# Sixteen up pairs of the first MLP by seven products instead of fifteen, with half of the factor sums' operands in PSUM

## The chip, the cores and the metric

The kernel runs on one core of one Trainium2 chip. The metric is the device time of one execution in microseconds (us), the median of several runs. Lower is better. The kernel is a hand-scheduled program: every engine has its own instruction list, and the lists are tied together by semaphores alone.

## The reference, cut to what matters

Three transformer layers run over 512 tokens of width 1024, in float32. The change touches the up projection of the first layer's MLP:

```
h2 = rms_norm(x, ffn_norm)                             # 512 x 1024
u = causal_dwconv(h2 @ w_up, conv_w, conv_b)           # w_up 1024 x 5632, three taps along the tokens
a, bval = jnp.split(u, 2, axis=-1)                     # 2816 + 2816 columns
return x + (jax.nn.silu(a) * bval) @ w_down            # w_down 2816 x 1024
```

Everything is computed with float32 accuracy. Each operand is split into a high and a low part (fp32r), and a product is the sum high x high + high x low + low x high: three matmuls for one.

## The kernel before

The 2816 columns of `a` and the 2816 of `bval` make 22 *pairs* of 128-column tiles (one tile of `a`, one of `bval`). Activations lie transposed, 128 features on the partitions and 512 tokens along the free axis.

**Plain pairs.** The first `N_PLAIN` = 7 pairs run as two ordinary tiles each (`up_tile`): 8 blocks of 128 features x 3 matmuls of 512 columns, 48 matmuls a pair. The weight tile arrives by DMA in `stage`, ScalarE (ACT) copies it to `w_hi` (L1791), GpSimd (POOL) subtracts to get `w_lo` (L639), VectorE (DVE) multiplies the result by `rstd` (`scaled`, L2890), ACT applies the first convolution tap (`conv_0_of`, L2055), and DVE the other two (`conv`, L2897 and L2900).

**Pairs by seven products.** The other `Q_UP` = 15 pairs use Strassen's scheme (Winograd's form) on 2 x 2 blocks: the pair's two tiles are the rows, two halves of the 1024 features the inner blocks, two halves of the tokens (256 each) the columns. `up_product(q, k)` runs one of the seven products, in the order `UP_ORDER` = A11, S1, A12, S2, S4, A22, S3: 4 feature blocks x 3 matmuls of 256 columns, so 12 matmuls a product and 84 a pair. Some products accumulate in the PSUM region of an earlier one, so they wait for ACT to copy that region away: S2 for `p1_copied` (L2094), S4 for `p5_copied` (L2101), S3 for `u2_copied` (L2107). DVE then adds the pieces (`c_00`, `c_01` at L2981, `c_1` at L2988).

**Factors.** The activation side of the seven products, the *factors* (four blocks B11, B12, B21, B22 of the normed input and sums T1 to T4 of them; seven of the eight are used), is made once during the plain pairs, in four *columns* k = 0 to 3, at the plain pairs i in `FACTORS_AT = [0, 1, 3, 4]`. For each column DVE computes blocks and sums (`factors_first`, `factors_second`), ACT copies them to the high parts (`factor_highs`), and DVE and POOL subtract to get the low parts (both have a `factor_lows`). After the last column DVE makes the weight sums of the first product pair (`up_sum`, L2947 and on).

**Weights of the product pairs.** Pair q's raw weights (two loads of 512 KB) go to `stage` for odd q and to other buffers for even q. The load of pair q waits for POOL's low part of A22 of pair q - 2.

**Hand-over to the down projection.** After the last pair the down projection uses `stage` again. Its first loads wait as this line says (L604):

```
sp.wait_ge(slot_low, UP_LOW_AT[HI_A22, Q_UP - 1 - (Q_UP % 2)])
loads(T_DOWN1, T_QKV[0])
```

In the last pair's turn, ACT's list has the high part of the first down tile (`down_split_hi(T_DOWN1)`, L2131) ahead of `p5_copied`, and that of the second down tile and three parts `f_high` (L2122) ahead of `u2_copied`. The down projection's first output tile (d = 0) takes its operands as they are finished: high parts first, then POOL's low parts of the down tiles (L762), then DVE's low parts of the MLP's hidden values (`f_low`, L2996).

Of the kernel before, what the change touches and what calls it, by code (L numbers as in the profile page):

```python
# [16 lines left out]
F32 = mybir.dt.float32  # L17
F32R = mybir.dt.float32r
ALU = mybir.AluOpType
# [3 lines left out]
S = 512  # L23
# [28 lines left out]
N_PLAIN = 7  # L52
# [27 lines left out]
FACTORS = [F_B11, F_T1, F_B21, F_T2, F_B22, F_T3, F_T4]  # L80
N_HIGH = N_PROD + 1
# [30 lines left out]
F_FREE = [F_B11, F_T1, F_B21, F_T2, F_B22, F_T4, F_T3]  # L112
# [60 lines left out]
def program(nc, x_in, params, consts, buckets, swa_table, weights, pairs, tables, out):  # L173
    with ExitStack() as ctx:
# [138 lines left out]
        SUM_X, SUM_Y = TR[1], OB  # L313

# [318 lines left out]
        def _(pool):  # L633
# [90 lines left out]
            def factor_lows(k):  # L724
# [4 lines left out]
                if k < QUADS - 1:  # L729
                    nc.gpsimd.tensor_tensor(factor[:, F_T1:, 1, ks], e[:, 2 * S:].rearrange("p (c s) -> p c s", c=4),  # L730
                                            factor[:, F_T1:, 0, ks].bitcast(F32), ALU.subtract).then_inc(factor_low, 1)
                    return
                nc.gpsimd.tensor_tensor(factor[:, F_T1, 1, ks], e[:, 2 * S:2 * S + HS], factor[:, F_T1, 0, ks].bitcast(F32),
                                        ALU.subtract).then_inc(factor_low, 1)
                if N_PLAIN - 2 in FACTORS_AT:
                    up_low(HI_A11, 0)
                nc.gpsimd.tensor_tensor(factor[:, F_T3:, 1, ks], e[:, 2 * S + HS:].rearrange("p (c s) -> p c s", c=3),
                                        factor[:, F_T3:, 0, ks].bitcast(F32), ALU.subtract).then_inc(factor_low, 1)
# [120 lines left out]
        def _(pe):  # L859
# [409 lines left out]
            def up_product(q, k):  # L1269
# [3 lines left out]
                f = FACTORS[k]  # L1273
# [10 lines left out]
                elif k == HI_S1:  # L1284
                    if q == 0:
                        pe.wait_ge(factor_low, QUADS)
                    else:
                        pe.wait_ge(product_added, 4 * (q - 1) + C_01)
                elif k == HI_A12 and q:
                    pe.wait_ge(product_added, 4 * (q - 1) + C_10)  # L1290
                elif k == HI_S2:
                    pe.wait_ge(up_moved, moved_at(q, P1_COPY))
                    if q == 0:
                        pe.wait_ge(factor_low, X_LOWS)
                elif k == HI_S4:
                    pe.wait_ge(up_moved, moved_at(q, P5_COPY))
                elif k == HI_A22:
                    pe.wait_ge(product_added, 4 * q + C_00)
# [485 lines left out]
        def _(act):  # L1784
# [261 lines left out]
            root(1)  # L2046
            def conv_0_of(i, p_):
# [15 lines left out]
            def factor_highs(k):  # L2063
# [3 lines left out]
                act.activation(factor[:, F_B11, 0, ks], factor_parts[k % 2][:, 0:HS], ACT.Copy).then_inc(ffh_ready, 1)  # L2067
                act.activation(factor[:, F_B21:, 0, ks], factor_parts[k % 2][:, S:].rearrange("p (c s) -> p c s", c=6),
# [1702 lines left out]
```

## Time and profile before

| | us |
|---|---|
| median of 3 runs (lowest to highest) | 1697.94 (1697.69 to 1698.26) |
| the profiled execution's own time | 1697.71 |
| its span, first to last instruction | 1695.6 |
| PE (TensorE matmul) busy | 1687.2 of 1695.6 |
| PEld (weight loads) busy | 1458.4 |
| DVE / ACT / POOL busy | 1135.2 / 901.3 / 1024.6 |

The profile is one execution. An engine's busy time counts the instructions that do work. Matmuls overlap one another in the profile, so the time that one really costs is the distance between two starts, not its own duration. The granted TensorE clock is 0.999 of full speed over the span.

### The profile page before, as it was taken

What the parts mean: (1) busy time and instruction counts of PE and PEld (TensorE: products, weight loads), DVE (VectorE), ACT (ScalarE), POOL (GpSimd) and SP (SyncE); (2) the same over time, 40 slices, a digit from 0 to 9 for tenths busy, and PEclk for the clock granted to TensorE, in tenths of its full rate; (3) what the DMA queues carried; (4) which work ended last, traced back from release to release, by engine and by line L of the source; (5) the groups of instructions that cost most, each with busy time, mean ns of one, the idle gap of its engine ahead of it and who ended that gap; (6) DMA issues with size and microseconds to landing.
All of it is one profiled execution on the core that took longest, in us unless ns stands there. A gap on an engine that the chain in (4) does not pass through costs nothing.

```text
span 1695.6 us, 28204 instructions
## 1 busy us (share of the span) xinstructions
PE 1687.2 (100%) x9959; PEld 1458.4 (86%) x9959; DVE 1135.2 (67%) x2222; ACT 901.3 (53%) x1643; POOL 1024.6 (60%) x1077
## 2 busy tenths in 40 slices
PE   9999999999999999999999999999999999999998
PEld 7778889999888888888989898977777889898988
DVE  6875788887411455667766666777777675757576
ACT  6665546787423444335454544656565454535355
POOL 6543688778554443357575757755554666666666
PEclk9999999999999999999999999999999999999999
DMA  5222343322234322223323233232331243333332
GB/s 196 74 69 63 100 125 103 110 100 88 87 100 143 97 69 84 75 87 112 112 88 112 89 111 92 98 125 84 119 106 50 88 136 100 100 100 99 101 99 76
DMA packets 48523, 168.22 MB, mean 99 GB/s; under 512 B 5216, under 2 KB 6512, under 8 KB 48400
## 3 DMA queue, kind: packets, MB, share of 16 engines
q1 hardware_dynamic: 48112, 166.08, 30.6%
q8 instruction: 73, 1.20, 0.3%
q10 hardware_dynamic: 288, 0.53, 0.1%
q14 instruction: 50, 0.41, 0.1%
HBM read 164.35 MB, written 2.24 MB: 98 GB/s over the span
## 4 chain that ended last, share of the span: by engine, by line
PE 99%; DVE 0%; ACT 0%; issue 0%; DVEq 0%
PE bank L961 19%; PE bank L880 7%; PE bank L879 7%; PE bank L885 7%; PE bank L1729 6%; PE bank L1738 6%; PE bank L1730 6%; PE bank L1311 3%; PE bank L1304 3%; PE bank L1303 3%; PE bank L979 3%; PE bank L980 3%; PE bank L985 3%; PE bank L1362 2%; PE bank L1353 2%; PE bank L1355 2%
## 5 line engine op out<-in xcount | busy, mean ns | idle before, releaser
L639 POOL TENSOR_TENSOR w_lo<-stage,w_hi 128x256 fp32r<-128x256 f32 x664 | 528.2, 827 | 416.2 <-ACT w_hi L1791 218.2
L1791 ACT ACTIVATE w_hi<-stage 128x1024 fp32r<-128x1024 f32 x166 | 174.7, 1053 | 167.0 <-DMA stage<-weights 57.3
L880 PE MATMUL bank<-xn_lo,w_hi 128*128 128x512 f32 x544 | 211.7, 389 | 0.0
L879 PE MATMUL bank<-xn_hi,w_hi 128*128 128x512 f32 x544 | 211.7, 389 | 0.0
L961 PE MATMUL bank<-xn_hi,w_hi 128*128 128x512 f32 x464 | 188.8, 407 | 0.0
L961 PE MATMUL bank<-xn_lo,w_hi 128*128 128x512 f32 x464 | 181.8, 392 | 0.0
L3480 DVE TENSOR_TENSOR x_space<-x_space,bank 128x256 f32<-128x256 f32 (+1 forms) x217 | 96.9, 455 | 86.8 <-PE bank L1738 84.9
L1738 PE MATMUL bank<-arena 128*128 128x256 f32 x896 | 146.6, 283 | 0.0
L885 PE MATMUL bank<-xn_hi,w_lo 128*128 128x512 f32 x544 | 135.0, 389 | 0.0
L1729 PE MATMUL bank<-arena 128*128 128x256 f32 x512 | 128.8, 283 | 0.0
L1730 PE MATMUL bank<-arena 128*128 128x256 f32 x512 | 128.7, 283 | 0.0
L1738 PEld LDWEIGHTS bank<-arena 128*128 128x128 f32 x896 | 124.8, 192 | 0.0
L961 PE MATMUL bank<-xn_hi,w_lo 128*128 128x512 f32 x464 | 123.8, 398 | 0.0
L885 PEld LDWEIGHTS bank<-xn_hi,w_lo 128*128 128x128 f32 x544 | 102.1, 188 | 21.2
L880 PEld LDWEIGHTS bank<-xn_lo,w_hi 128*128 128x128 f32 x544 | 102.1, 188 | 21.1
L879 PEld LDWEIGHTS bank<-xn_hi,w_hi 128*128 128x128 f32 x544 | 102.2, 188 | 20.9
L3500 DVE TENSOR_TENSOR arena<-tmp,arena 128x256 fp32r<-128x256 f32 (+2 forms) x120 | 108.2, 922 | 3.8 <-ACT arena L2514 2.5
L961 PEld LDWEIGHTS bank<-xn_hi,w_hi 128*128 128x128 f32 x464 | 87.2, 188 | 22.9 <-issue 6.3
L961 PEld LDWEIGHTS bank<-xn_hi,w_lo 128*128 128x128 f32 x464 | 84.6, 188 | 21.7 <-issue 4.9
L961 PEld LDWEIGHTS bank<-xn_lo,w_hi 128*128 128x128 f32 x464 | 87.3, 188 | 16.0
L1729 PEld LDWEIGHTS bank<-arena 128*128 128x128 f32 x512 | 98.3, 192 | 0.1
L1730 PEld LDWEIGHTS bank<-arena 128*128 128x128 f32 x512 | 98.3, 192 | 0.0
(512 smaller groups left out, 4317.5 us busy)
## 6 DMA issues: line engine op xcount, KB each, us to landing
stage<-weights SPq DMA_DIRECT2D x189, 512.0 KB, 3.5
stage<-pairs SPq DMA_DIRECT2D x46, 512.0 KB, 3.6
prob<-pairs SPq DMA_DIRECT2D x32, 512.0 KB, 3.6
bias<-table SPq DMA_DIRECT2D x11, 896.0 KB, 5.5
xn_raw<-pairs SPq DMA_DIRECT2D x14, 512.0 KB, 4.4
out<-y SPq DMA_DIRECT2D x8, 256.0 KB, 2.3
x_space<-x_in SPq DMA_DIRECT2D x3, 512.0 KB, 7.3
bias<-swa_table SPq DMA_DIRECT2D x4, 256.0 KB, 3.7
```

What stands on the lines that cost most here:

```text
L639: ins = nc.gpsimd.tensor_tensor(w_lo[:, p_, ks], stage[:, p_, ks], w_hi[:, p_, ks].bitcast(F32), ALU.subtract)
L879: pe.matmul(G[p_][:], w_hi[:, p_, k], hi[:, k], start=(first and k == ks[0]), stop=False)
L880: mm = pe.matmul(G[p_][:], w_hi[:, p_, k], lo[:, k], start=False, stop=False)
L885: mm = pe.matmul(G[p_][:], w_lo[:, p_, k], hi[:, k], start=False, stop=(last and k == ks[-1]))
L961: mm = pe.matmul(G[p_][:], (w_hi if i < 2 * KD else w_lo)[:, p_, k], (xn_lo if i < 2 * KD and i % 2 else xn_hi)[:, k], start=(i == 0), sto ...
L979: pe.matmul(G[dd][:], w, ff_hi[:, k], start=(k == k0), stop=False)
L1729: pe.matmul(region, w, fc_hi[:, i, f], start=(fresh and i == 0), stop=False, skip_group_check=True)
L1730: pe.matmul(region, w, fc_lo[:, i, f], start=False, stop=False, skip_group_check=True)
L1738: mm = pe.matmul(region, w, fc_hi[:, i, f], start=False, stop=(i == QUADS - 1), skip_group_check=True)
L1791: act.activation(w_hi[:, p_], stage[:, p_], ACT.Copy).then_inc(hi_ready, 1)
L3480: dve.tensor_tensor(dst, dst, src, ALU.add).then_inc(product_added, 1)
L3500: dve.tensor_tensor(fc_lo[:, i, a:b + 1].rearrange("p c s -> p (c s)"), src, fc_hi[:, i, a:b + 1].rearrange("p c s -> p (c s)").bitcast(F3 ...
```

## The change

`N_PLAIN` goes from 7 to 6, so 16 pairs run by products and 6 plain. The plain stage, under which the factors are made, is one pair shorter, while `FACTORS_AT` stays. The making of the factors is rearranged:

- ACT copies `rstd` once to an idle PSUM bank (`ROOT`). DVE's blocks read it there.
- B12 (needed only on the way) and T1, T2 are written to PSUM (`B12`, `T12`) instead of SBUF, so that each block or sum has at most one tensor operand in SBUF. `T12` and `B12` are one buffer each, where the SBUF parts alternate between two.
- The factors lie in another order (`U_...`), with T1 and T2 first. DVE makes the low parts of T1, T2 and B11, POOL those of the other four. PE's waits on them move accordingly.

The diff, cut to its core:

```diff
-N_PLAIN = 7
+N_PLAIN = 6
+U_T1, U_T2, U_B11, U_B21, U_B22, U_T3, U_T4 = range(7)
+UP_FACTORS = [U_B11, U_T1, U_B21, U_T2, U_B22, U_T3, U_T4]
-F_FREE = [F_B11, F_T1, F_B21, F_T2, F_B22, F_T4, F_T3]
+F_FREE = [UP_FACTORS[k] for k in UP_ORDER]
+        ROOT, T12, B12 = MB, OB, TR[0][:, 0:HS]
...
             root(1)
+            act.wait_ge(rstd_ready, 2)
+            act.activation(ROOT[:], rstd[:], ACT.Copy)
...
             def factor_highs(k):
-                act.activation(factor[:, F_B11, 0, ks], factor_parts[k % 2][:, 0:HS], ACT.Copy).then_inc(ffh_ready, 1)
-                act.activation(factor[:, F_B21:, 0, ks], factor_parts[k % 2][:, S:].rearrange("p (c s) -> p c s", c=6),
+                act.activation(factor[:, U_T1:U_T2 + 1, 0, ks], T12.rearrange("p (c s) -> p c s", c=2), ACT.Copy).then_inc(ffh_ready, 1)
+                act.activation(factor[:, U_B11:, 0, ks], factor_parts[k % 2][:, 0:5 * HS].rearrange("p (c s) -> p c s", c=5),
                                ACT.Copy).then_inc(ffh_ready, 1)
...
             def factors_first(k):
-                dve.scalar_tensor_tensor(out=e[:, 0:S], in0=x[:, k], scalar=pcol("ffn_norm", k, k + 1), in1=rstd[:],
+                dve.scalar_tensor_tensor(out=b11, in0=x[:, k, 0:HS], scalar=pcol("ffn_norm", k, k + 1), in1=ROOT[:, 0:HS],
                                          op0=ALU.mult, op1=ALU.mult)
-                dlink(dve.scalar_tensor_tensor(out=e[:, S:2 * S], in0=x[:, k + 4], scalar=pcol("ffn_norm", k + 4, k + 5), in1=rstd[:],
+                dve.scalar_tensor_tensor(out=B12, in0=x[:, k, HS:S], scalar=pcol("ffn_norm", k, k + 1), in1=ROOT[:, HS:S],
+                                         op0=ALU.mult, op1=ALU.mult)
+                dlink(dve.scalar_tensor_tensor(out=e[:, HS:3 * HS], in0=x[:, k + 4], scalar=pcol("ffn_norm", k + 4, k + 5), in1=ROOT[:],
                                                op0=ALU.mult, op1=ALU.mult))
-                dve.tensor_tensor(t1, b12, b11, ALU.subtract)
-                dlink(dve.tensor_tensor(t3, b22, b12, ALU.subtract))
+                dve.tensor_tensor(t1, B12, b11, ALU.subtract)
+                dlink(dve.tensor_tensor(t3, b22, B12, ALU.subtract))
```

The wait of L604 is not in the diff, but its value follows from `Q_UP`. With 15 pairs it names pair 13; with 16 it names pair 15, the last, whose raw weights now lie in `stage`.

**DVE, the last factor column.** Before, the two blocks and the sums T1, T3, then `scaled`, then T2, T4, one more convolution (two rows of `tmp<-bank,par,tmp`), a `scaled`, and the low parts:

```order
L2916 SCALAR_TENSOR_TENSOR v_tok<-x_space,par,rstd 128x512 [waits factor_low,ff_ready,ffh_ready]
L2918 SCALAR_TENSOR_TENSOR v_tok<-x_space,par,rstd 128x512
L2920 TENSOR_TENSOR v_tok<-v_tok 128x256 [waits dve_chain]
L2921 TENSOR_TENSOR v_tok<-v_tok 128x256
L2890 TENSOR_TENSOR bank<-bank,rstd 128x512 [waits tile_done,dve_chain]
L2926 TENSOR_TENSOR v_tok<-v_tok 128x256
L2927 TENSOR_TENSOR v_tok<-v_tok 128x256 [waits dve_chain]
L2897 SCALAR_TENSOR_TENSOR tmp<-bank,par,tmp 128x511 [waits conv_0]
L2900 SCALAR_TENSOR_TENSOR tmp<-bank,par,tmp 128x510 [waits conv_1]
L2890 TENSOR_TENSOR bank<-bank,rstd 128x512 [waits tile_done]
L2933 TENSOR_TENSOR arena<-v_tok,arena 128x256 [waits ffh_ready]
L2936 TENSOR_TENSOR arena<-v_tok,arena 128x2x256 [waits ffh_ready]
```

The same place in the changed kernel:

```order
L2922 SCALAR_TENSOR_TENSOR v_tok<-x_space,par,bank 128x256 [waits factor_low,ff_ready,ffh_ready]
L2924 SCALAR_TENSOR_TENSOR bank<-x_space,par,bank 128x256
L2926 SCALAR_TENSOR_TENSOR v_tok<-x_space,par,bank 128x512
L2928 TENSOR_TENSOR bank<-bank,v_tok 128x256 [waits dve_chain]
L2929 TENSOR_TENSOR v_tok<-v_tok,bank 128x256
L2896 TENSOR_TENSOR bank<-bank,rstd 128x512 [waits tile_done,dve_chain]
L2934 TENSOR_TENSOR bank<-v_tok,bank 128x256
L2935 TENSOR_TENSOR v_tok<-v_tok,bank 128x256 [waits dve_chain]
L2941 TENSOR_TENSOR arena<-bank,arena 128x2x256 [waits ffh_ready]
L2944 TENSOR_TENSOR arena<-v_tok,arena 128x256 [waits ffh_ready]
L2954 TENSOR_TENSOR bank<-bank,arena_raw 128x512 [waits ff_ready,quad_full0,slot_high]
```

The first block is in two pieces, all sums have a bank among their operands, and the convolution and `scaled` that stood between the sums and the low parts now come after the weight sums, whose first is the last row.

**ACT, the third factor column.** Before, its high parts (the two rows of `arena`) stand ahead of the next weight tile's high part:

```order
L2055 ACTIVATE tmp<-bank,par 128x512 [waits f_made,up_moved]
L2067 ACTIVATE arena<-arena_raw 128x256 [waits factor_made]
L2068 ACTIVATE arena<-arena_raw 128x6x256
L1791 ACTIVATE w_hi<-stage 128x1024 [waits hi_free,stage_full0]
L2055 ACTIVATE tmp<-bank,par 128x512 [waits f_made,up_moved]
```

In the changed kernel they stand behind it:

```order
L2061 ACTIVATE tmp<-bank,par 128x512 [waits f_made,up_moved]
L1795 ACTIVATE w_hi<-stage 128x1024 [waits hi_free,stage_full0]
L2073 ACTIVATE arena<-bank 128x2x256 [waits factor_made]
L2074 ACTIVATE arena<-arena_raw 128x5x256
L2061 ACTIVATE tmp<-bank,par 128x512 [waits f_made,up_moved]
```

So these high parts wait for the weight tile, too.

**SP, the loads from the last product pairs to the first down tiles.** Before (`stage<-pairs` and `xn_raw<-pairs` are the raw weights of odd and even pairs, the branch carries the wait of L604):

```order
L597 DMA stage<-pairs 128x1024 [waits slot_low]
L597 DMA stage<-pairs 128x1024
L597 DMA xn_raw<-pairs 128x1024 [waits slot_low]
L597 DMA xn_raw<-pairs 128x1024
L507 UNCONDITIONAL_BRANCH [waits slot_low]
L507 ISA
L504 ISA [waits lo_ready]
L504 DMA stage<-weights 128x1024
```

In the changed kernel:

```order
L600 DMA xn_raw<-pairs 128x1024 [waits slot_low]
L600 DMA xn_raw<-pairs 128x1024
L600 DMA stage<-pairs 128x1024 [waits slot_low]
L600 DMA stage<-pairs 128x1024
L510 UNCONDITIONAL_BRANCH [waits slot_low]
L510 ISA
L507 ISA [waits lo_ready]
L507 DMA stage<-weights 128x1024
```

The last pair's loads now go to `stage`, right ahead of the down tiles that take the same buffer.

## Rows read from the trace of the kernel before

**Rows 1.** The page's span, and the chain that ended last, by engine.

```profile
span 1695.6 us, 28204 instructions
...
PE 99%; DVE 0%; ACT 0%; issue 0%; DVEq 0%
```

**Rows 2.** Timeline of PE (start, duration): last plain pair's start, first product's start.

```profile
261.72 0.39 PE L1261 MATMUL bank<-xn_hi,w_hi 128*128 128x512 f32 x1
...
272.60 0.28 PE L1303 MATMUL bank<-arena,bias_slots 128*128 128x256 f32 x1
```

**Rows 3.** Timeline of PE: first matmuls of product pairs 3, 4 and 14 (the last).

```profile
302.83 0.28 PE L1303 MATMUL bank<-arena,bias_slots 128*128 128x256 f32 x1
...
312.91 0.28 PE L1303 MATMUL bank<-arena,bias_slots 128*128 128x256 f32 x1
...
413.71 0.28 PE L1303 MATMUL bank<-arena,bias_slots 128*128 128x256 f32 x1
```

**Rows 4.** Timeline of DVE, from the last factor column to the first product.

```profile
249.59 1.30 DVE L2916 SCALAR_TENSOR_TENSOR v_tok<-x_space,par,rstd 128x512 f32<-128x512 f32 x1
...
252.64 0.84 DVE L2920 TENSOR_TENSOR v_tok<-v_tok 128x256 f32<-128x256 f32 x1
...
255.96 2.51 DVE L2927 TENSOR_TENSOR v_tok<-v_tok 128x256 f32<-128x256 f32 x1
...
261.37 1.78 DVE L2936 TENSOR_TENSOR arena<-v_tok,arena 128x512 fp32r<-128x512 f32 x1
...
265.11 0.69 DVE L2947 TENSOR_TENSOR bank<-bank,arena_raw 128x512 f32<-128x512 f32 x1
...
272.80 0.70 DVE L2890 TENSOR_TENSOR bank<-bank,rstd 128x512 f32<-128x512 f32 x1 [0.27 <-PE bank L1266]
```

**Rows 5.** Timeline of ACT, from the third factor column to the first product pair.

```profile
244.69 1.47 ACT L2068 ACTIVATE arena<-arena_raw 128x1536 fp32r<-128x1536 f32 x1
246.38 1.06 ACT L1791 ACTIVATE w_hi<-stage 128x1024 fp32r<-128x1024 f32 x1 [0.22 <-DMA stage<-weights]
...
277.08 0.38 ACT L2101 ACTIVATE bank<-bank 128x256 f32<-128x256 f32 x1
```

**Rows 6.** Timeline of POOL: the last low part it makes before the first product.

```profile
270.82 1.29 POOL L745 TENSOR_TENSOR v_split<-arena_raw,v_split 128x512 fp32r<-128x512 f32 x1
```

**Rows 7.** The first two down loads: SP's timeline; line L504's and L597's landings; SP's waits.

```profile
404.72 0.88 SPq L504 DMA_DIRECT2D stage<-weights  x2
...
DMA to landing us min/median/max: 4.6/4.9/5.3
...
DMA to landing us min/median/max: 3.5/4.0/4.5
...
SPq L507 <- POOL xn_hi L745: 8.7, 1, 8.7
```

**Rows 8.** Timeline of ACT in the last product pair.

```profile
416.29 1.06 ACT L2131 ACTIVATE arena<-stage 128x1024 fp32r<-128x1024 f32 x1
418.05 0.37 ACT L2101 ACTIVATE bank<-bank 128x256 f32<-128x256 f32 x1 [0.70 <-issue]
418.33 1.05 ACT L2131 ACTIVATE arena<-stage 128x1024 fp32r<-128x1024 f32 x1
...
420.84 0.38 ACT L2107 ACTIVATE rstd<-bank 128x256 f32<-128x256 f32 x1
```

**Rows 9.** Timelines of DVE, of POOL and of PE behind it; PE's wait there.

```profile
421.25 0.43 DVE L2981 TENSOR_TENSOR bank<-rstd,bank 128x256 f32<-128x256 f32 x1 [2.54 <-ACT rstd L2107]
...
424.41 0.43 DVE L2988 TENSOR_TENSOR bank<-xn_raw,bank 128x256 f32<-128x256 f32 x1 [0.19 <-ACT xn_raw L2113]
...
429.52 4.63 POOL L762 TENSOR_TENSOR bias_slots<-stage,bias_slots 128x256 fp32r<-128x256 f32 x4
...
434.24 1.63 PE L1362 MATMUL bank<-arena,bias_slots 128*128 128x512 f32 x6
...
PEld bank L1362 <- POOL bias_slots L762: 0.2, 1, 0.2
```

More of the change, by code:

```diff
@@ L729, in factor_lows @@
                 if k < QUADS - 1:
[L730 to L731 removed]
+                    nc.gpsimd.tensor_tensor(factor[:, U_B21:, 1, ks], e[:, HS:5 * HS].rearrange("p (c s) -> p c s", c=4),
+                                            factor[:, U_B21:, 0, ks].bitcast(F32), ALU.subtract).then_inc(factor_low, 1)
                     return
[L733 to L734 removed]
+                nc.gpsimd.tensor_tensor(factor[:, U_B21:U_B22 + 1, 1, ks], e[:, HS:3 * HS].rearrange("p (c s) -> p c s", c=2),
+                                        factor[:, U_B21:U_B22 + 1, 0, ks].bitcast(F32), ALU.subtract).then_inc(factor_low, 1)
                 if N_PLAIN - 2 in FACTORS_AT:
                     up_low(HI_A11, 0)
[L737 to L738 removed]
+                nc.gpsimd.tensor_tensor(factor[:, U_T3:, 1, ks], e[:, 3 * HS:5 * HS].rearrange("p (c s) -> p c s", c=2),
+                                        factor[:, U_T3:, 0, ks].bitcast(F32), ALU.subtract).then_inc(factor_low, 1)
             def up_low(k, q):
@@ L1284, in up_product @@
                 elif k == HI_S1:
+                    if q:
+                        pe.wait_ge(product_added, 4 * (q - 1) + C_01)
+                elif k == HI_A12:
                     if q == 0:
@@ L1287, in up_product @@
                     else:
-                        pe.wait_ge(product_added, 4 * (q - 1) + C_01)
-                elif k == HI_A12 and q:
-                    pe.wait_ge(product_added, 4 * (q - 1) + C_10)
+                        pe.wait_ge(product_added, 4 * (q - 1) + C_10)
                 elif k == HI_S2:
                     pe.wait_ge(up_moved, moved_at(q, P1_COPY))
-                    if q == 0:
-                        pe.wait_ge(factor_low, X_LOWS)
                 elif k == HI_S4:
@@ L1297, in up_product @@
                 elif k == HI_A22:
+                    if q == 0:
+                        pe.wait_ge(factor_low, X_LOWS)
                     pe.wait_ge(product_added, 4 * q + C_00)
@@ L2905, in parts @@
                 e = factor_parts[k % 2]
-                return [e[:, c * HS:(c + 1) * HS] for c in range(8)]
+                return [e[:, c * HS:(c + 1) * HS] for c in range(5)] + [T12[:, 0:HS], T12[:, HS:S]]
             def factors_first(k):
                 e = factor_parts[k % 2]
+                b11, b21, b22, t3, t4, t1, t2 = parts(k)
                 if k >= 2:
@@ L2932, in factor_lows @@
                 dve.wait_ge(ffh_ready, 2 * k + 1)
-                dve.tensor_tensor(factor[:, F_B11, 1, ks], e[:, 0:HS], factor[:, F_B11, 0, ks].bitcast(F32),
+                dve.tensor_tensor(factor[:, U_T1:U_T2 + 1, 1, ks], T12.rearrange("p (c s) -> p c s", c=2),
+                                  factor[:, U_T1:U_T2 + 1, 0, ks].bitcast(F32), ALU.subtract).then_inc(ff_ready, 1)
+                dve.wait_ge(ffh_ready, 2 * k + 2)
+                dve.tensor_tensor(factor[:, U_B11, 1, ks], e[:, 0:HS], factor[:, U_B11, 0, ks].bitcast(F32),
                                   ALU.subtract).then_inc(ff_ready, 1)
-                dve.wait_ge(ffh_ready, 2 * k + 2)
-                dve.tensor_tensor(factor[:, F_B21:F_T1, 1, ks], e[:, S:2 * S].rearrange("p (c s) -> p c s", c=2),
-                                  factor[:, F_B21:F_T1, 0, ks].bitcast(F32), ALU.subtract).then_inc(ff_ready, 1)
             def up_sum(q, k):
```

8 lines of the change are left out of this document (3 added, 5 removed).

## The prediction

> **What bounds the kernel now.** I read the page first. The chain that ended last is PE at 99% [rows 1]: matmul follows matmul almost without a gap. So a change can gain only by what it takes out of PE's own list, and it loses whatever it makes PE wait. Next I read PE's timeline for the price of the two kinds of pair, then the timelines of DVE, ACT and POOL at the two seams: from the plain pairs to the products (around 272.6 us), and from the last pair to the down projection (from 413.7 us). Those are the only places where the order around PE changes.
>
> **What PE's list gains.** The last plain pair starts at 261.72 and the first product at 272.60 [rows 2]: 10.88 us for 48 matmuls, 0.227 us each. A pair by products goes from 302.83 to 312.91 [rows 3]: 10.08 us for 84 matmuls, 0.120 us each. One pair changes kind, so PE's list is 0.80 us shorter. This is all that can be gained.
>
> The Trainium skill (page "TensorE: Matmul & The Clock Gate", section "Back-to-back issue gap") gives N / 2.4 + 2.5 ns for an isolated matmul of N columns at full clock. By it a plain pair is 48 x 215.8 ns and a product pair 84 x 109.2 ns, and the gain would be 10.36 - 9.17 = 1.19 us. The trace's spacings are wider, above all for 256 columns (120 against 109 ns), so the measured 0.80 decides. The same section warns that at smaller N the spacing also carries the weight load, which is what the rows look like.
>
> **Seam 1, plain pairs to products.** Products would now start at 261.72 instead of 272.60, 10.88 us sooner, while the last factor column still belongs to plain pair 4. In the kernel before, DVE started on that column at 249.59, ended its low parts at 261.37 + 1.78 = 263.15, made the first weight sum at 265.11, and was done with the work behind it so that it waited 0.27 us for PE at 272.80 [rows 4]. Left as it was, the column would be ready only after the products want it.
>
> The new column costs less. A 256-wide sum with both operands in SBUF took 0.84 and even 2.51 us [rows 4]; one with a bank among its operands took 0.43 [rows 9]. So four sums take 1.7 us. The blocks (two of 256, one of 512) I take at about 0.45 + 0.45 + 0.75, an estimate from 0.43 for 256 and 0.70 for 512 with a bank operand [rows 4, 9]. With the `scaled` between them (0.7) and about 0.2 for the links, 249.59 leads to about 253.8 for the finished sums; before it was 255.96 + 2.51 = 258.47. ACT's first high part (some 0.6 for 512 columns) and DVE's low part (0.7) follow, then ACT's second part and DVE's low part of B11. That puts the first weight sum at about 255.6 to 256.5, and it is earlier still if the column starts sooner than 249.59. The start is set by the high parts of the third column: they now stand behind a weight tile's copy that waits until PE has freed `w_hi`. That is PE's second half of pair 4, near 243.3 by PE's pace, so they run from about 244.4 to 246.2, against 244.69 + 1.47 = 246.16 before [rows 5]. The order change there costs nothing, and the column starts at about 248.5 to 249.6. I take 255.3 for the first weight sum, 6.4 us ahead of the first product; before it was 272.60 - 265.11 = 7.5 ahead. DVE is thus 1.1 later against PE (bounds 0.6 and 1.8).
>
> Who waits for it? After the sums DVE has the same work as before until the last `scaled`. That one had 0.27 to spare, so it is 0.8 late. ACT's copy for S4 ended at 277.08 + 0.38 = 277.46 [rows 5], 4.86 us after the first product's start; S4 starts 4 x 12 x 0.120 = 5.76 after it. That is 0.90 of cover for 0.8 of delay: cost 0, with bounds 0 and 0.8. POOL's last low part before the first product, for S4, ended at 270.82 + 1.29 = 272.11 [rows 6]; in the changed kernel I expect it 1 to 2 us behind the first product, and S4's low matmuls want it 6.7 behind: cost 0. The copy of `rstd` to the bank (ACT, 0.6) delays a weight tile that PE wants only after two plain tiles: cost 0. Fewer sums in SBUF also take less of POOL's time, which helps only engines that are not the bound.
>
> **Seam 2, last pair to the down projection.** The first two down loads go to `stage`. With 15 pairs they waited for pair 13's A22, that is, they were released one pair early: issued at 404.72 [rows 7], which is 1.09 after pair 13's start (413.71 - 10.08 = 403.63). SP was waiting for just this POOL operation [rows 7]. With 16 pairs the wait names the last pair. Call its start T: the loads leave at T + 1.09. Those two landed 4.6 and 5.3 after issue [rows 7], so the first is there at T + 5.7.
>
> ACT's list holds the copy of that tile ahead of the copy for S4. Before, it ran at 416.29, T + 2.58 [rows 8]. Now it runs at T + 5.7, 3.1 later, and the next instruction on ACT starts about 0.95 behind it, at T + 6.65. The 0.37 of `p5_copied` [rows 8] brings T + 7.05. S4 wanted it at T + 5.76: **PE stalls 1.3 us**.
>
> Next is S3, which waits for `u2_copied`. That stood 420.84 - 418.05 = 2.79 behind `p5_copied` [rows 8], so it runs from T + 9.45 to T + 9.85. S3 starts at 8.64 + 1.3 = T + 9.94: no further stall. But DVE's `c_01`, at 421.25 or T + 7.54 before [rows 9], moves to T + 9.9, 2.4 later. `c_1`, which had 0.19 to spare [rows 9], is 2.2 later, and behind it stand the last convolution, the last hidden value and POOL's low part of the third down tile (429.52 + 4.63 = 434.15 [rows 9]). PE already waited 0.2 for that part at 434.24 [rows 9], so there is no cover left, and the whole 2.2 arrives at PE. It contains the 1.3: **seam 2 costs 2.2 us in total**. Bounds: if the load lands after 3.5, the least that a pair's load took [rows 7], everything is 1.1 less, so 1.1; at 5.3 it is 2.9. Below, no bound but 0, if ACT's list had room.
>
> **The sum.** -0.80 + 0 + 2.2 = +1.4 us. The profiled execution took 1697.71 us, 2.1 more than its span; it would take 1699.1. The median of the runs shown is 0.23 higher, so I forecast 1699.3. That is 0.08% slower: below the 0.2% (3.4 us) that a measurement of this kernel can tell from no change.
>
> **The rivals.**
> *The hand-over is hidden* (chance 0.18). The loads land quickly, or ACT and DVE catch up, and the stall is 1.1 or less: -0.80 to +0.3, 1697.1 to 1698.2. For it: fast landings of 3.5 occur. Against: the loads of this very place took 4.6 and more, and PE's cover behind it was 0.
>
> *The factors come late* (0.15), which ends slower. This is one mechanism: the last column's chain DVE, ACT, DVE does not shrink as estimated, because B11's low part still has both operands in SBUF, the links between dependent sums cost more, or the third column's high parts run later than 246.2. If nothing shrank, the first weight sum would come some 9 + 3 us after 249.59, near 262, 7.8 later against PE than before, and the stall would be 7.8 - 0.27 - 0.90 = 6.6: 1706. It decides (slower by over 3.4 together with seam 2) when seam 1 costs over 2.0, when the first weight sum comes later than about 257.4. For it: the 2.51 of one sum [rows 4]. Against: 0.43 for each operation with a bank [rows 9].
>
> The Trainium skill (page "SBUF — State Buffer", section "SBUF: two separate sides") says that DVE with two SBUF inputs and GpSimd exclude each other for a whole instruction. By that rule the new sums are free of POOL, but B11's low part is not and can wait out one POOL instruction.
>
> *Faster by over 0.2%* (0.02): PE's list gives 0.80, and no wait of PE that the change could remove is near 2.6 us.
>
> **How the numbers follow.** My forecast (seam 2 between 1.1 and 2.9, seam 1 below 1) has 0.62, from +0.3 to +3.1 us. Both small costs together reaching the bound without passing it have 0.03. Within 0.2%: 0.62 + 0.18 + 0.03 = 0.83; slower 0.15, faster 0.02. The range leaves out little of the hidden case at the bottom (1697.2) and reaches a step into late factors at the top (1702.0).
>
> **What the profile of the changed kernel would show.** Right: first product at 261.7 to 262; product pairs 10.08 apart; first weight sum near 255.3; S4 of the last pair starting 7.1 instead of 5.8 us after the pair's first matmul, with ACT idle before the first L2137 until a DMA; PE waiting at the third down tile's low part for 0.9. Wrong: a gap at the first products' S1, A12 or S4 (factors late), ACT's first down copy at T + 3 to T + 4.5 (load hidden), or a PE wait in between that no row of before shows.

## The result, and the profile after

| | before | changed |
|---|---|---|
| median, us (lowest to highest, 11 runs each) | 1698.01 (1697.69 to 1699.52) | 1701.56 (1700.89 to 1703.05) |
| profiled execution's own time / its span | 1697.71 / 1695.6 | 1701.56 / 1699.8 |

The ratio is 1.002, with a 95% interval of 1.0012 to 1.0028. The change makes the kernel 3.55 us slower, which is 0.21%, right at the 0.2% that the measurement can tell from no change. The forecast was 1699.3, in a range of 1697.2 to 1702.0, with 0.83 for a difference within 0.2% and 0.15 for slower; the measured one lies on that border.

The page of the changed kernel: its span, the busy times, and the chain that ended last, by engine.

```profile
span 1699.8 us, 28304 instructions
...
PE 1688.0 (99%) x9995; PEld 1459.8 (86%) x9995; DVE 1128.0 (66%) x2234; ACT 907.8 (53%) x1654; POOL 1020.6 (60%) x1074
...
PE 96%; DVE 1%; ACT 1%; DMA 1%; POOL 0%; issue 0%; DVEq 0%; SPq 0%; ACTq 0%; POOLq 0%
```

DVE has 7 us less to do than before, and PE's share of the chain has fallen from 99% [rows 1] to 96%: the chain now leaves PE for DVE, ACT and a DMA. So PE waits where it did not. PE's timeline (start, duration, and in brackets the idle time before the row with what ended it) shows where. First the seam from plain tiles to products; S2 starts at 267.15 and S4 at 269.51.

```profile
262.32 0.28 PE L1307 MATMUL bank<-arena,bias_slots 128*128 128x256 f32 x1
...
267.15 0.36 PE L1307 MATMUL bank<-arena,bias_slots 128*128 128x256 f32 x1 [0.36 <-ACT rstd L2100]
...
269.51 0.36 PE L1307 MATMUL bank<-arena,v_split 128*128 128x256 f32 x1 [0.69 <-ACT bank L2107]
```

Then the last pair (its first matmul, and S4's), and the low part of the third down tile:

```profile
415.17 0.28 PE L1307 MATMUL bank<-arena,bias_slots 128*128 128x256 f32 x1
...
422.33 0.36 PE L1307 MATMUL bank<-arena,v_split 128*128 128x256 f32 x1 [1.24 <-ACT bank L2107]
...
438.30 1.65 PE L1366 MATMUL bank<-arena,bias_slots 128*128 128x512 f32 x6 [0.70 <-POOL bias_slots L765]
```

Distances between first matmuls, read from PE's timelines of both kernels (good to about 0.01), give this account. T is the start of the last pair, d = 0 and d = 1 are the down projection's output tiles.

| | before | changed | difference |
|---|---|---|---|
| last plain pair against a pair by products | 10.88 | 10.08 | -0.80 |
| place where the products (before: the last plain pair) start | 261.72 | 262.32 | +0.60 |
| pair 0 | 10.08 | 11.57 | +1.49 |
| pair 1 | 10.08 | 10.24 | +0.16 |
| pairs 2 to the last but one, each | 10.08 | 10.08 | 0 |
| last pair, T to down projection | 10.08 | 11.54 | +1.46 |
| d = 0 to d = 1 | 15.12 | 16.25 | +1.13 |

The sum is +4.04 (4.06 by the two starts of d = 1; the rest is rounding); the spans differ by 4.2. The 0.60 looks like scatter: three profiles of the kernel before have the first product at 272.60, 272.78 and 273.02, which less 10.88 is 261.72 to 262.14, and all the kernels here with six plain pairs have it between 261.70 and 262.46. Without it 3.44 remain, and the medians differ by 3.55. Seam 1 costs 1.65 and seam 2 2.59, against a gain of 0.80.

**Seam 1 in the changed kernel.** DVE's timeline, to be held against [rows 4]: the first sum and the last, the low parts of T1 and T2, that of B11, the first weight sum, and the last `scaled`.

```profile
250.95 0.43 DVE L2928 TENSOR_TENSOR bank<-bank,v_tok 128x256 f32<-128x256 f32 x1
...
252.80 0.42 DVE L2935 TENSOR_TENSOR v_tok<-v_tok,bank 128x256 f32<-128x256 f32 x1
253.89 0.69 DVE L2941 TENSOR_TENSOR arena<-bank,arena 128x512 fp32r<-128x512 f32 x1 [0.67 <-ACT arena L2073]
255.05 2.19 DVE L2944 TENSOR_TENSOR arena<-v_tok,arena 128x256 fp32r<-128x256 f32 x1 [0.47 <-ACT arena L2074]
257.37 0.70 DVE L2954 TENSOR_TENSOR bank<-bank,arena_raw 128x512 f32<-128x512 f32 x1
...
264.71 0.69 DVE L2896 TENSOR_TENSOR bank<-bank,rstd 128x512 f32<-128x512 f32 x1
```

POOL's timeline over the same microseconds, and ACT's copy for S4:

```profile
254.55 2.40 POOL L733 TENSOR_TENSOR arena<-arena_raw,arena 128x1024 fp32r<-128x1024 f32 x1
```

```profile
268.98 0.38 ACT L2107 ACTIVATE bank<-bank 128x256 f32<-128x256 f32 x1
```

The sums are as cheap as forecast (0.43, 0.42), and they end at 253.2. But B11's low part, a 256-wide operation whose two operands both lie in SBUF, took 2.19 us. It started 0.50 after a POOL instruction of 2.40 us and ended 0.29 after it. The first weight sum then comes 262.32 - 257.37 = 4.95 ahead of the first product; it was 7.49 before, and 6.4 in the forecast. (Two of the kernels below leave this place as it is: there the same row took 2.18 and 2.17, and pair 0 11.54 and 11.55.) The last `scaled` is 264.71 - 262.32 = 2.39 behind the first product, where it was 0.20 [rows 4]. That is 2.19 late. The copy for S4 ends 7.04 behind, where it was 4.86 [rows 5]: 2.18 late, against a cover of 0.90. The 1.28 that is left, and 0.1 to 0.2 for PE's restart, make the 1.49.

**Seam 2 in the changed kernel.** SP's timeline of the first two down loads, and their landings (line L507 between 415 and 420):

```profile
416.25 0.88 SPq L507 DMA_DIRECT2D stage<-weights  x2
...
DMA to landing us min/median/max: 4.6/4.9/5.3
```

ACT's timeline, to be held against [rows 8], and DVE's (`c_1`, and two low parts of hidden values) and POOL's (the second down tile's low part, and the third's) behind it, against [rows 9]:

```profile
420.85 1.06 ACT L2137 ACTIVATE arena<-stage 128x1024 fp32r<-128x1024 f32 x1 [2.98 <-DMA stage<-weights]
421.81 0.37 ACT L2107 ACTIVATE bank<-bank 128x256 f32<-128x256 f32 x1
...
424.62 0.36 ACT L2113 ACTIVATE rstd<-bank 128x256 f32<-128x256 f32 x1
```

```profile
427.97 0.42 DVE L2995 TENSOR_TENSOR bank<-xn_raw,bank 128x256 f32<-128x256 f32 x1
...
428.63 1.84 DVE L3003 TENSOR_TENSOR arena<-arena_raw,arena 128x512 fp32r<-128x512 f32 x2
```

```profile
426.03 3.29 POOL L765 TENSOR_TENSOR arena<-stage,arena 128x256 fp32r<-128x256 f32 x4
...
433.63 4.62 POOL L765 TENSOR_TENSOR bias_slots<-stage,bias_slots 128x256 fp32r<-128x256 f32 x4
```

The loads leave at T + 1.08, ACT's down copy starts at T + 5.68, the copy for S4 at T + 6.64, and S4 itself at T + 7.16. `c_1` is at T + 12.80 instead of T + 10.70, 2.10 late, and POOL's low part of the third tile ends at T + 23.08 instead of T + 20.44, 2.64 late. DVE's row between them accounts for the other 0.54. In the kernel before it read

```profile
425.08 1.29 DVE L2996 TENSOR_TENSOR arena<-arena_raw,arena 128x512 fp32r<-128x512 f32 x2
```

and stood behind the end of POOL's second low part (424.78). Now it starts before that end (426.03 + 3.29 = 429.32) and takes 1.84 instead of 1.29: the first of its two instructions, with both operands in SBUF, takes 1.23 instead of 0.69. It is the same meeting as at seam 1. No run takes this one away by itself.

### The profile page after: what moved, and what is told of

The parts are those of the page before. It is cut to its first block, busy times and chain, and to the rows that moved or that the text cites. A ratio compares the mean times of both kernels' runs of the same rounds, so it can differ in the third digit from the quotient of the medians.

```text
span 1699.8 us, 28304 instructions
## 1 busy us (share of the span) xinstructions
PE 1688.0 (99%) x9995; PEld 1459.8 (86%) x9995; DVE 1128.0 (66%) x2234; ACT 907.8 (53%) x1654; POOL 1020.6 (60%) x1074
## 4 chain that ended last, share of the span: by engine, by line
PE 96%; DVE 1%; ACT 1%; DMA 1%; POOL 0%; issue 0%; DVEq 0%; SPq 0%; ACTq 0%; POOLq 0%
PE bank L964 19%; PE bank L883 7%; PE bank L882 7%; PE bank L888 7%; PE bank L1733 6%; PE bank L1742 6%; PE bank L1734 6%; PE bank L1307 3%; PE bank L1315 3%; PE bank L1308 3%; PE bank L982 3%; PE bank L988 3%; PE bank L983 3%; PE bank L1366 2%; PE bank L1359 2%; PE bank L1357 2%
## 5 line engine op out<-in xcount | busy, mean ns | idle before, releaser
L642 POOL TENSOR_TENSOR w_lo<-stage,w_hi 128x256 fp32r<-128x256 f32 x656 | 519.6, 824 | 418.7 <-ACT w_hi L1795 212.3
```

Source lines behind the costliest of these rows:

```text
L642: ins = nc.gpsimd.tensor_tensor(w_lo[:, p_, ks], stage[:, p_, ks], w_hi[:, p_, ks].bitcast(F32), ALU.subtract)
```

## The experiments

Eight edited kernels and two further profiles of the kernel before. Times are medians. The experiments ran on three chips, and each ratio is against runs of the kernel before on the same chip: its medians there were 1698.66 (25 runs), 1698.38 (27) and 1698.94 (13). Medians from different chips are compared with care. The runs of the kernel before lie mostly in two groups, around 1697.9 and around 1699.3, on every chip. What makes the two groups is the last experiment's subject.

### The two halves of the change apart

The rearranged factors without the 16th pair:

```diff
-N_PLAIN = 6
+N_PLAIN = 7
```

> The changed kernel with seven plain pairs again, so only the factor sums are rearranged. My theory: both seams keep the cover that they had in the kernel before (a plain pair of 10.88 us more at the first, the down loads released a pair early at the second), so the time is that of the kernel before within 0.3 us, and the first weight sum stands more than 8 us ahead of the first product. Rival: part of the loss comes from the rearranged factors themselves (the copy to the bank, single buffers for T1, T2 and B12); then this kernel is slower than the kernel before by 1 us or more.

Measured: 1697.82 (1697.60 to 1697.95, 10 runs), ratio 0.9997 (0.9988 to 1.0007). Every pair is 10.08, the first weight sum stands 10.07 ahead of the first product, the down projection starts 10.08 behind T and d = 0 takes 15.08. So rearranging the factors costs nothing by itself.

The 16th pair with the old factors (the kernel before with `N_PLAIN = 6`):

> The kernel before with six plain pairs, the factors as before. My theory: the last factor column, slowed by POOL, is late by some 6 us at the first product pair, the second seam costs the same 2.6 us as in the changed kernel, PE's list gives 0.8: slower than the kernel before by about 8 us, and the last pair's S4 still starts about 7.2 us after the pair's first matmul. Rival: operands in PSUM buy little, and the time is that of the changed kernel, +3.5 us.

Measured: 1707.73 (1706.76 to 1708.30, 4 runs), ratio 1.0054 (1.0038 to 1.0071). Pair 0 takes 16.55, pair 1 10.95, and seam 2 is as in the changed kernel (S4 at T + 7.16, down projection at T + 11.55, d = 0 16.26). The longest wait is on ACT's copy, in PE's timeline:

```profile
271.73 0.55 PE L1303 MATMUL bank<-arena,bias_slots 128*128 128x256 f32 x1 [3.56 <-ACT bank L2076]
```

Seam 1 loses 7.3 us with the old factors and 1.65 with the new ones. In these two profiles the rearrangement as a whole (operands in PSUM, and the convolution moved behind the weight sums) is thus worth 5.7 us at seam 1. No run parts the two, and the 7.3 contains some 2.3 us of a meeting of DVE and POOL that not every execution has; it is shown under the last experiment. The forecast's price for "nothing shrank" was 6.6, without a term for the clock, and the clock did fall. Behind the wait of 3.56 the stretch from 271.7 to 274.6 reads (PE busy, granted clock, DMA share, GB/s):

```profile
271.70:274.60 2.90, 2.87 (x13) 0.50 0.01 3
```

The clock is 1.00 from 262 to 271 and 0.50, the 1.2 GHz level, in this stretch. S2 took 2.70 instead of 1.44 there. Most of that covers the next wait, for ACT's copy for S4 ended at 273.98 and S4 started at 274.43; my estimate from these rows is that the slow clock costs 0.4 of the 7.3. In the changed kernel the clock reads 1.00 across both seams, where PE's longest idle time was 1.24.

### Seam 2 without seam 1

The kernel before with `N_PLAIN = 8`: 14 pairs, an even number as 16 is, so the last pair lies in `stage` again, while the factors have more room than before.

> The kernel before with eight plain pairs and fourteen by products, the factors as before. Nothing is late at the first seam. The last product pair is again one whose weights lie in the stage buffer, so the down loads are released in the last pair. My theory: PE's list is 0.8 us longer and the second seam costs 2.6 us: +3.4 us, with S4 of the last pair starting near 7.1 us instead of 5.8 after the pair's first matmul. Rival: the second seam's cost has to do with there being sixteen pairs, not with the buffer; then +0.8 us and S4 at 5.8.

Measured: 1702.06 (1700.07 to 1703.46, 10 runs), ratio 1.002 (1.001 to 1.0029). All pairs before the last are 10.08. In the profiled execution (1700.24) the loads landed sooner, after a median of 4.0, and ACT's row reads

```profile
419.52 1.06 ACT L2131 ACTIVATE arena<-stage 128x1024 fp32r<-128x1024 f32 x1 [2.08 <-DMA stage<-weights]
```

With T = 414.74 that is T + 4.78. S4 started at T + 6.26, the down projection at T + 10.64, and d = 0 took 16.28. Seam 2 needs an even number of product pairs and nothing else of the change. Its size goes with the landings: it is 1.72 here, where the first load landed after 3.7, 2.59 in the changed kernel (4.6), and 2.87 in the next experiment's (4.9). The median of this kernel is +3.4, as I expected, but its profile accounts for 0.80 + 1.72 only. It fell on one of the three quick runs (1700.07 to 1700.24); the other seven took 1702.0 to 1703.5, and what makes them longer no profile shows.

### POOL's long instruction in pieces

In the changed kernel POOL's low parts of a factor column's last four factors are one 1024-wide instruction. Here they are four of 256:

```diff
-                    nc.gpsimd.tensor_tensor(factor[:, U_B21:, 1, ks], e[:, HS:5 * HS].rearrange("p (c s) -> p c s", c=4),
-                                            factor[:, U_B21:, 0, ks].bitcast(F32), ALU.subtract).then_inc(factor_low, 1)
+                    for c in range(4):
+                        ins = nc.gpsimd.tensor_tensor(factor[:, U_B21 + c, 1, ks], e[:, (1 + c) * HS:(2 + c) * HS],
+                                                      factor[:, U_B21 + c, 0, ks].bitcast(F32), ALU.subtract)
+                    ins.then_inc(factor_low, 1)
```

> The changed kernel, with POOL's low parts of the first three factor columns in four instructions of 256 columns instead of one of 1024. My theory: DVE's low part of B11 in the last column took 2.19 us because POOL's 1024-wide instruction was running; it now gets in after a quarter and takes 1.1 us or less, the first weight sum comes 1.0 to 1.5 us earlier, and the first product pair takes 10.1 to 10.5 us instead of 11.57: 1.0 to 1.4 us less than the changed kernel. Rival: POOL goes from one quarter to the next without letting DVE in; then the instruction still takes about 2.2 us and nothing changes.

Measured: 1700.12 (1698.37 to 1701.02, 10 runs), ratio 1.0006 (0.9996 to 1.0016). Timelines of POOL and DVE:

```profile
254.68 3.01 POOL L734 TENSOR_TENSOR arena<-arena_raw,arena 128x256 fp32r<-128x256 f32 x4
```

```profile
255.19 0.51 DVE L2946 TENSOR_TENSOR arena<-v_tok,arena 128x256 fp32r<-128x256 f32 x1 [0.47 <-ACT arena L2076]
255.83 0.70 DVE L2956 TENSOR_TENSOR bank<-bank,arena_raw 128x512 f32<-128x512 f32 x1
```

DVE's instruction has the same operands, and POOL works for 3.01 us beside it, yet it took 0.51 instead of 2.19 (0.52 in both other kernels with the pieces). The first weight sum comes 262.46 - 255.83 = 6.63 ahead of the first product. Pair 0 takes 10.07. So the 1.49 of pair 0 is this one instruction. Seam 2 is here 2.87, for the loads landed after 4.9 and 5.6; the profiled execution was the slowest of the ten. Pair 1 now takes 10.64, and the row that explains it is ACT's:

```profile
274.01 0.60 ACT L2084 ACTIVATE bank<-xn_raw 128x512 f32<-128x512 f32 x1 [0.90 <-DMA xn_raw<-pairs]
```

This copy takes pair 2's raw weights, and the copy for S4 stands behind it on ACT. The changed kernel has the same wait (0.47 there).

### The down projection's first load released sooner

The first down tile goes to the half of `stage` that the last pair's POOL low part of A12 and DVE's sum for S4 read last; here it is released by those two, and only the second tile's load by A22:

```diff
-            sp.wait_ge(slot_low, UP_LOW_AT[HI_A22, Q_UP - 1 - (Q_UP % 2)])
-            loads(T_DOWN1, T_QKV[0])
+            sp.wait_ge(slot_low, UP_LOW_AT[HI_A12, Q_UP - 1])
+            sp.wait_ge(sum_made, N_SUM * (Q_UP - 1) + UP_SUM[HI_S4])
+            load(T_DOWN1 // 2, 0)
+            sp.wait_ge(slot_low, UP_LOW_AT[HI_A22, Q_UP - 1])
+            load(T_DOWN1 // 2, 1)
+            loads(T_DOWN1 + 2, T_QKV[0])
```

> The changed kernel, with the load of the first down tile released by what really reads its half of the buffer last (the low part of A12 and the sum S4 of the last pair), about 3 us before A22's low part, which still releases the second tile. My theory (the late load is the cause at the second seam): ACT's first down copy runs at about 2.6 us after the last pair's start T instead of 5.7, S4 starts at T + 5.76, and what stays of the seam is the second tile's load, 0 to 1.2 us; 1.4 to 2.6 us less than the changed kernel, whose first seam is unchanged (first product pair 11.6 us). Rival (ACT's list is simply too full in the last pair, whatever the load does): S4 still starts after T + 6.5.

Measured: 1699.82 (1698.82 to 1700.44, 10 runs), ratio 1.0009 (0.9999 to 1.0018). The first load leaves 2.3 ahead of T = 415.74 instead of 1.1 behind it, and ACT's down copy starts at T + 2.59, as before the change:

```profile
413.42 3.44 SPq L507 DMA_DIRECT2D stage<-weights  x2
```

```profile
418.33 1.06 ACT L2141 ACTIVATE arena<-stage 128x1024 fp32r<-128x1024 f32 x1
```

S4 starts at T + 5.76, the down projection at T + 10.08, and d = 0 takes 15.06: all of seam 2 is gone. The two loads now left 3.1 apart, and landed after 3.4 and 3.5. The span is only 1.8 shorter than the changed kernel's, because pair 1 lost 1.38 here, to the same wait for pair 2's load (1.71 on ACT).

### ACT's order in the last pair

The other way out of seam 2 leaves the loads where they are and puts ACT's two down copies behind `p5_copied` and `u2_copied`:

```diff
                     conv_0_of(i - 1, 1)
-                    if not more:
-                        down_split_hi(T_DOWN1)
...
                 else:
-                    down_split_hi(T_DOWN1 + 1)
-                    for f in range(N_EARLY, 11):
-                        f_high(f)
+                    f_high(N_EARLY)
                 u2_copied(q)
+                if not more:
+                    down_split_hi(T_DOWN1)
+                    down_split_hi(T_DOWN1 + 1)
+                    for f in range(N_EARLY + 1, 11):
+                        f_high(f)
```

(`f_high` 11 and 12 move behind `u3_copied`.)

> The changed kernel, load and first seam untouched, with ACT's list in the last pair turned round: the copies for S4 and S3 stand ahead of both down tiles' copies, three hidden values' high parts move behind the pair's last copy. My theory (the load hurts only through what is queued behind it): S4 starts at T + 5.76 although the load lands at T + 5.7, the last convolution is about 0.7 us late instead of 2.2, and the whole seam costs 0.5 to 1.0 us instead of 2.6: 1.6 to 2.1 us less than the changed kernel. Rival: the work that ACT has put off arrives late at the down projection, and the loss only moves from S4 to the first down tiles; then the seam still costs 2 us or more.

Measured: 1700.80 (1700.06 to 1701.36, 10 runs), ratio 1.0013 (1.0003 to 1.0022). S4 starts at T + 5.76 and the down projection at T + 10.08, so the stall of S4 did come from ACT's order. But d = 0 takes 16.77 instead of 15.12, more than I expected; PE waits for POOL's low part of the third down tile:

```profile
437.80 1.67 PE L1366 MATMUL bank<-arena,bias_slots 128*128 128x512 f32 x6 [1.11 <-POOL bias_slots L765]
```

The work that was put off came late. Seam 2 costs 1.65 this way, against 2.59 in the changed kernel and nothing with the sooner load. The loads landed sooner in this profile (3.6 and 4.3), and ACT's two down copies started only at T + 6.24, so a landing of 4.6 would have cost nothing more here. Against the 1.72 that the old order costs with a landing of 3.7, the new order gains next to nothing; by this estimate it helps only when the loads are slow. The two medians, not measured side by side, are 0.8 apart.

### Everything that the profiles pointed to, together

POOL's pieces and the sooner down load as above; `u2_copied` and one `f_high` ahead of ACT's second down copy; and pair 2's load no longer waits for POOL's low part of A22 of pair 0, because its buffer `xn_raw` is free as soon as the plain tiles are done, which the load waits for anyway:

```diff
-                elif q >= 2:
+                elif q >= 3:
                     sp.wait_ge(slot_low, UP_LOW_AT[HI_A22, q - 2])
                 if q == 2:
                     sp.wait_ge(tile_done, T_DOWN1)
```

> The changed kernel with all three pieces: POOL's factor lows in quarters, the first down tile's load released early, ACT's copy for S3 ahead of the second down tile's copy, and the load of pair 2 released by the end of the plain tiles (its buffer has no other reader before), which should take away the 0.6 us that the quarters kernel still lost in pair 1. My theory: no wait is left at either seam and only the 0.80 us of PE's list remains: about 1697.2, a span near 1694.9, every product pair 10.08 us, the end of the last pair to the second down output 15.1 us. Rival: something that no trace has shown yet becomes the bound, and the time stays at or above the kernel before.

Measured: 1696.97 (1696.79 to 1697.33, 11 runs), ratio 0.999 (0.9981 to 0.9999). Every pair takes 10.08, the down projection starts at T + 10.08, d = 0 takes 15.08, and PE waits at neither seam. (The sooner down load alone had already emptied seam 2, so ACT's new order isn't shown to be needed.) SP's timeline shows pair 2's load 0.2 behind the first product (262.08), where the changed kernel issued it at 270.17, 7.85 behind:

```profile
262.28 0.81 SPq L600 DMA_DIRECT2D xn_raw<-pairs  x2
```

The same kernel without that last edit:

> The version with the quartered GpSimd product, the earlier release of the down projection's first loads and the reordered ScalarE copies, but with the load of pair 2's input operands released again where the changed kernel releases it. Theory: the second pair's loss comes from that load alone: pair 0 stays at 10.08, pair 1 measures 10.3 to 11.4 with ScalarE's copy of pair 2's rows ending an idle time on the DMA, everything behind it is as in the covered version (seam 2 without a stall, down projection 10.08 after the last pair's start), so the median is 0.2 to 1.3 above it, 1697.2 to 1698.3. Rival: the reordering did it, and the load's release is worth nothing: every pair 10.08 and 1697.0.

Measured: 1698.22 (1697.55 to 1698.84, 10 runs), ratio 0.9997 (0.9987 to 1.0007). The profile is of the quickest run (1697.55): pair 0 10.07, pair 1 10.39, all else as in the covered version, and ACT's copy waits:

```profile
273.32 0.60 ACT L2088 ACTIVATE bank<-xn_raw 128x512 f32<-128x512 f32 x1 [0.63 <-DMA xn_raw<-pairs]
```

The load left at 268.23, 5.1 ahead of that copy's start. So pair 1's loss is this load's release. Its ten runs are 1.3 us wide, and the covered version's eleven lie within 0.54, which suggests that most of that width goes with it. The medians are 1.25 apart, on different chips, of which the profile accounts for 0.31.

### The two groups of the kernel before

> The kernel before once more, for a second profile. Theory: its two groups of times (near 1697.9 and near 1699.2) differ at the seam from plain tiles to products, where ScalarE's copy waits for the load of pair 2's operands: a profile with a span near 1696.9 shows pair 1 at 11 to 11.6 instead of 10.08 and ScalarE idle before its copy until a DMA; one with a span near 1695.6 shows none of it. Rival: the 1.3 us lie elsewhere (the start of the kernel, the down projection), and all pairs read 10.08 in both.

> The same kernel a third time, for a further profile, with the same two expectations: either pair 1 reads 11 to 11.6 with a span near 1696.9, or every pair 10.08 with a span near 1695.6; the rival has every pair at 10.08 whatever the span.

One profile fell in each group: 1697.71 with a span of 1695.8, and 1699.23 with 1697.3. In the first every pair is 10.08. In the second pair 0 takes 11.23 and pair 1 10.20, and all else is equal. It is seam 1, as I expected, but the load that I blamed is not the cause: ACT has no wait for a DMA there. DVE's timelines (first the execution of the lower group, then that of the upper) differ in the third factor column:

```profile
238.64 1.38 DVE L2916 SCALAR_TENSOR_TENSOR arena_raw<-x_space,par,rstd 128x512 f32<-128x512 f32 x1
...
265.23 0.69 DVE L2947 TENSOR_TENSOR bank<-bank,arena_raw 128x512 f32<-128x512 f32 x1
```

```profile
238.82 4.03 DVE L2916 SCALAR_TENSOR_TENSOR arena_raw<-x_space,par,rstd 128x512 f32<-128x512 f32 x1
...
267.76 0.69 DVE L2947 TENSOR_TENSOR bank<-bank,arena_raw 128x512 f32<-128x512 f32 x1
```

One block with both tensor operands in SBUF took 4.03 instead of 1.38, and the first weight sum is 2.5 late. POOL's timeline of the upper execution has no gap beside it:

```profile
235.44 5.61 POOL L639 TENSOR_TENSOR w_lo<-stage,w_hi 128x256 fp32r<-128x256 f32 x8
241.01 1.29 POOL L751 TENSOR_TENSOR arena_raw<-tmp 128x512 f32<-128x512 f32 x1
```

The block started at 238.82 and ended at 242.85, 0.55 behind the end of POOL's last row (242.30); a block that doesn't wait takes 0.75. Between those times POOL finished five instructions, four of 0.74 and one of 1.29, and this time none of the first four ends let DVE in. In the first profile of this program (span 1695.6) the same block took 0.75, beside the same POOL instructions. With the rearranged factors alone this block reads `rstd` in PSUM, and its ten runs lie within 0.35 us, all in the lower group. In the seven profiles with rearranged factors every block and sum of all four columns takes its own time to 0.01 us (0.47, 0.48 and 0.74; 0.41 to 0.43), whatever POOL does beside it. A single profile of the upper group doesn't prove that every run of it is of this kind.

A second execution shows the same thing, though: the profile of the old factors with six plain pairs, on DVE's timeline.

```profile
238.59 4.08 DVE L2916 SCALAR_TENSOR_TENSOR arena_raw<-x_space,par,rstd 128x512 f32<-128x512 f32 x1
```

So two of the five profiles with the old factors have it. Counted from the first product, the first weight sum is 2.29 later in the upper execution than in the lower one (5.26 ahead instead of 7.55). Without it I estimate seam 1 with the old factors at about 5.0 instead of 7.3, and the rearrangement's worth at 3.4 instead of 5.7.

## Why the prediction was right in direction, and what it mis-sized

The direction was right, the time lies inside the range, and the reason held: PE's list gains 0.80, and the hand-over to the down projection loses more. The forecast was +1.4 and the measured difference +3.55. By its own steps:

- **PE's list, -0.80: right.** Pairs by products that wait for nothing are 10.08 in every kernel. The covered version, with the gain and no stall, took 1696.97, and the rearranged factors alone 1697.82. That is 0.85 apart, but on different chips; their profiles are 0.55 apart at the first matmul of d = 1 and 0.3 in span, for the products began 0.25 late in the covered one. The Trainium skill's formula for isolated matmuls (page "TensorE: Matmul & The Clock Gate", section "Back-to-back issue gap") would have given an estimate of 1.19 for the same step, which the spacings here do not show.
- **The sums' price, about 0.45 each: right** (0.41 to 0.43), and so were the blocks (0.47, 0.48, 0.74). The rearrangement saves 5.7 us at seam 1 between two profiles, or 3.4 by estimate without the meeting of 4.08 us.
- **Seam 1, cost 0 with bounds 0 and 0.8: the step that failed.** "I take 255.3 for the first weight sum, 6.4 us ahead of the first product." It came at 257.37, 4.95 ahead, and the seam cost 1.65. With POOL's instruction in pieces it comes 6.63 ahead and pair 0 costs nothing, so everything else in this step held, and the 1.68 between 6.63 and 4.95 is B11's low part waiting behind POOL's 2.40 us. The rival "factors come late" named just this instruction, but the sum priced it as if it ran alone, and set the bound to 0.8. The step's own rule for the cost was sound: 7.49 - 4.95 = 2.54 of delay, less 0.27 and 0.90, is 1.37, against 1.49 in pair 0. The section "SBUF: two separate sides" of the Trainium skill's page "SBUF — State Buffer" says that such a DVE instruction can wait out one POOL instruction; the trace agrees, with 2.19 against 0.51, so its rule should have gone into the sum. In two profiles with the old factors a wait outlasted five POOL instructions (4.03 and 4.08 us), more than the page says, and there the measurement decides.
- **Pair 2's load: not foreseen.** It is released by POOL's low part of A22 of pair 0, so each delay of the DVE chain moves it too. It left 7.85 behind the first product, where the kernel before had 278.28 - 272.60 = 5.68. It cost 0.16 in the profile of the changed kernel, and 0.31 to 1.38 in profiles of the edited ones.
- **Seam 2, 2.2 with bounds 1.1 and 2.9: right in mechanism, 2.59 in size.** Loads at T + 1.08 (forecast 1.09), first down copy at T + 5.68 (5.7), copy for S4 at T + 6.64 (6.65), S4 at T + 7.16 (7.05), `c_1` 2.1 late (2.2). The rest is POOL's low part, which ended 2.64 late instead of 2.2: DVE's low part beside POOL's second one took 0.55 longer, the same kind of meeting that the sum left out at seam 1. That the cause is the buffer of an even number of pairs is shown by the kernel with 14; that it is the release and not the landing, by the sooner load that removes all of it.
- **The hand-over is hidden: did not happen** in any profile with an even number of pairs and the old release, though a quick landing (3.7, with 14 pairs) brought S4's delay down from 1.40 to 0.50.
- **The 0.6 at the start** of the products looks like scatter, which no step had; the medians hardly contain it.
- **The range held with some luck.** The scenario that had 0.62 ended at +3.1, or 1701.0. The result is above it, and inside the range only because the top reached a step into "factors come late". Of the signs named beforehand, one of the wrong ones came, a gap at S4 of the first product pair, beside the right ones at the last pair.

## What to carry to other kernels

When a stage moves earlier against a chain on other engines, list every instruction of that chain whose operands all lie in SBUF, and price each with at least one whole GpSimd instruction of those that run beside it. Cutting up the largest one removed the wait here, in three profiles, but an unbroken run of short ones held VectorE off in two others. The blocks and sums with an operand moved to PSUM waited in no profile. When a count changes parity, check each wait that names a buffer by it: the same line then releases a transfer one stage later. A transfer released late is best cured at the release: reordering its consumer removed the first stall and left another, and releasing it sooner removed both.

## What the runs showed of the hardware that was not expected

- A 256-wide VectorE instruction with both tensor operands in SBUF took 2.19 us beside one GpSimd instruction of 2.40 us, and 0.51 beside four that together took 3.01. Cutting the GpSimd work cost 0.6 us on GpSimd and let VectorE in behind the first piece.
- That is no rule: one such instruction of 512 columns took 0.75 and 1.38 us in two executions and 4.03 in a third of the same program, where it outlasted five GpSimd instructions in a row, four of them of only 0.74. The third has its first product pair 1.15 longer. The version with six plain pairs shows it once more, with 4.08. In ten runs with one operand moved to PSUM, no run fell in the upper group of times.
- Two loads of 512 KB issued 0.6 apart landed after 3.6 to 4.9 (the first) and 4.3 to 5.7 us (the second) in nine profiles; issued 3.1 to 3.3 apart, in three more, each landed after 3.4 to 3.6. Seam 2 grew from 1.72 to 2.87 us as the first landing went from 3.7 to 4.9.
- With one operand in PSUM, all blocks and sums of the factors took 0.41 to 0.48 us (256 columns) or 0.74 (512) in seven profiles. In the kernel before, the same work took 0.43 to 2.51 (sums) and 0.74 to 4.03 (blocks).
- TensorE's granted clock read 0.50 (the 1.2 GHz level) for about 2.9 us right behind an idle time of 3.56 us, and stayed at 1.00 behind idle times of 1.24 and 1.52.
